# A one-core decoder step: the last tile's output projection in three banks, two weight homes freed by halves, and one expert matrix loaded later

## The chip, the cores and the metric

The kernel runs on one core of a Trainium2 chip. The metric is the time of one execution on the device in microseconds; the time of the kernel before is the median of three executions. Beside it there is one profiled execution, from which all rows below come.

## What is computed

One layer of a decoder step for 256 prompt tokens and 8 sample tokens, all in fp32. A combined input projection feeds a gated convolution, a sparse attention with an indexer, and a cross-attention; their gated sum goes through the output projection `w_o`. After that, with the 264 tokens as three row tiles (128, 128 and 8):

```
h = LN(alpha*h + mixer(h));   h = LN(alpha*h + HierMoE(h))

def hier_moe(x, w_group, b_group, w_expert, b_expert, w_up, w_down):
    lg = xt @ w_group + b_group;  le = xt @ w_expert + b_expert      # 4 groups, 8 experts in each
    # best group by lg, two best experts in it by le, gate = softmax weights; every other gate is 0
    for e in range(N_EXPERTS):                                       # 32
        hu = xt @ w_up[e]                                            # 1024 -> 2*256
        y = y + gate[:, e:e + 1] * ((silu(hu[:, :256]) * hu[:, 256:]) @ w_down[e])
```

The weights of the experts are 32 x (2 MiB up + 1 MiB down) = 96 MiB, all of which are read once.

## The kernel before, in words

**Stages.** From 0 to some 317 us of the profile the branches, the gates and the sparse attention run. Then comes the output projection with the first layer norm and the routing (some 317 to 359 us), then the experts in eight groups of four, called quads (359 to 550 us), then the second layer norm and the stores.

**Output projection.** `wo_first` multiplies tile 0 into banks 0 and 1 beside the last branch tiles. `wo_second(dh, ks)` (L1042) multiplies tile 1 (the last tile of prompt tokens) by 512 columns of `w_o` into bank 2 (dh 0) or bank 3 (dh 1), for the blocks k in `ks`; its pieces are put between the work for tiles 0 and 2 in an order written out by hand (L1071 to L1111). A finished piece raises `wo_ps`; at 3 and 4 VectorE forms h for one half of tile 1 (`residual`, L2389), at `r_ready` 3 and 4 TensorE turns it (`r_turn`, L1048), four blocks of 128 columns at a time into banks 5 and 6, and ScalarE copies it to SBUF (`h_turned`, L1680). The logits of the router for tile 1 are summed from the turned blocks (L1105 to L1108), and `lg_ps` 2 tells VectorE so.

**Routing.** VectorE takes statistics of h, centres it (`ln_centre`), forms the logits (`logit`, L2394) and the choice of experts (`route`, L2455), and scales h into the transposed store `hturn` (`ln_scale_turned`, L2379). TensorE then counts, with the matrices "tri" and ones, at which position of its expert each token stands (L1125 to L1127) and the total of each expert (L1129, six instructions), and signals both with one `pos_ps` 2. VectorE turns the positions into the gather matrix of quad 0 (`places`, `first_slots`, L2514 to L2516), takes the largest total (L2517, `cnt_read`), scales h for the residual (`ln_scale`, L2518, `h_ready` 3), and prepares the gates; `e_ready` starts ScalarE's exp (L1701), behind which on ScalarE's queue stand the two copies of gathered tokens (L1721, `first_sb` 1 and 2) that quad 0 needs. TensorE gathers with `first_part` (L1118 is its matmul; 32 instructions before the counts, 16 after), waits for `cnt_read` (L1136) and starts quad 0.

**Homes and their order.** Weight units of 2 MiB go to NWS = 10 homes in SBUF. `UNITS` is their order, six units for each quad (four up, two down); entry p lies in home p % 10. The down weights of experts 0 and 1 have no home: they lie aside, expert 1 in `down_1`, expert 0 in the halves `down_0[0]` and `down_0[1]`, three transfers that raise `aside_in` to 48. SP issues all of them in one loop (L535 on), in program order, each behind its waits. For p >= 10 the wait is `used_w`, the number of units that TensorE has used up (L562). In quad 0 home 0 and home 1 are used together by `up_half(0, 0)` (four steps r, L1209 on) and are free at the end of step 3; homes 2 and 3 by `up_half(0, 1)`. Entry 10 (two down matrices of quad 1) goes to home 0 and entry 11 (an up matrix of quad 2) to home 1. Before entry 10 SP waits for `route_ready` and issues `down_0[1]` (L559). From quad 2 to 6 the up units are whole experts, so their four homes come free only at the end of all 64 instructions of the quad's up pass.

**Quad 0 on TensorE** (L1371 on): `up_half(0, 0)`, `up_half(0, 1)`, `residual_tile(1)`, `gate_turn`, two gathers, `mid_turn`, then `down(0)` (matmuls at L1364), which waits for `aside_in` 48 (L1353) among others, then gathers, `up(1)`, and so on; `up(2)` is the L1218 pass that ends near 417 us.

The lines that the steps below touch:

```
L556  sp.dma_start(down_0[0], e0[:, 0]).then_inc(aside_in, 16)
L558  if p == NWS:
L559      sp.wait_ge(route_ready, 1)
L560      sp.dma_start(down_0[1], e0[:, 1]).then_inc(aside_in, 16)
L561  if p >= NWS:
L562      sp.wait_ge(used_w, SPENT[units[p - NWS]])
```

## Time and profile before

| | us |
|---|---|
| median of 3 runs | 571.61 |
| the three runs | 571.61, 571.46, 576.95 |
| the profiled execution | 572.16 |
| its span (what the profile covers) | 570.3 |
| granted TensorE clock, mean | 0.97 of full speed |

Engines over the span: TensorE busy 92%, VectorE 47%, ScalarE 19%, GpSimd 8%; DMA moved 162.47 MB, 285 GB/s on average. All times of rows count from the span's start. A granted clock of 1.00 is 2.4 GHz, 0.50 is 1.2 GHz. Busy shares of TensorE come from modelled ends and say little on how hard it works. MiB and KiB are powers of two (as the "KB" of the DMA answers), GB/s are decimal.

### The profile page before, as it was taken

To read this page: it belongs to the slowest core of one execution; us is meant where nothing else is said; L and a number is where in the kernel's file an instruction comes from. 1 tells how busy PE (TensorE), PEld (TensorE's weight loads), DVE (VectorE), ACT (ScalarE), POOL (GpSimd) and SP (SyncE) were. 2 spreads that over 40 slices of the span, in tenths; PEclk is the share of its full clock that TensorE was granted. 3 is DMA by queue.
4 is the path that set the end of the run, shared out by engine and by line. 5 is a ranking of instruction groups with operands and counts; after the bars stand their busy time and mean duration, and the time that the engine had idled before them with its cause. 6 is when DMAs were issued, how large, how long until landed. Compare 5 with 4: busy or idle time off the path is not lost.

```text
span 570.3 us, 9541 instructions
## 1 busy us (share of the span) xinstructions
PE 527.6 (92%) x3941; PEld 321.3 (56%) x3941; DVE 266.6 (47%) x791; ACT 107.7 (19%) x253; POOL 48.2 (8%) x64
## 2 busy tenths in 40 slices
PE   8999999998999999999999998999999795948894
PEld 4555456474577778887776557555655251512332
DVE  1272753898889976864652696411002000100016
ACT  1001112011323534322000331111111010100123
POOL 0000000001011435320000000000000000002000
PEclk9999999999999999999999998999999897989987
DMA  8990442944293568744889957799999999999972
GB/s 299 401 347 8 147 148 63 383 151 151 76 332 111 186 213 285 240 163 155 347 342 411 311 183 296 257 431 419 426 423 430 419 427 421 431 421 421 402 239 79
DMA packets 48338, 162.47 MB, mean 285 GB/s; under 512 B 6274, under 2 KB 25180, under 8 KB 39076
## 3 DMA queue, kind: packets, MB, share of 16 engines
q1 hardware_dynamic: 39472, 138.76, 62.8%
q0 software_dynamic: 3728, 14.33, 7.2%
q10 hardware_dynamic: 5092, 8.74, 4.5%
q8 instruction: 33, 0.54, 0.4%
q14 instruction: 13, 0.11, 0.1%
HBM read 159.02 MB, written 2.77 MB: 284 GB/s over the span
## 4 chain that ended last, share of the span: by engine, by line
PE 64%; DMA 14%; DVE 13%; ACTq 5%; issue 2%; ACT 1%; SPq 0%; POOLq 0%; POOL 0%; DVEq 0%
PE bank L654 14%; PE bank L833 13%; DMA ring<-in_w_up 13%; PE bank L1218 7%; PE bank L601 4%; PE bank L1248 3%; PE bank L1364 2%; ACTq L1665 2%; ACTq L1664 2%; PE bank L1188 2%; PE bank L1170 2%; DVE ring L1889 2%; DVE gates L2022 2%; PE bank L670 2%; PE bank L1287 1%
## 5 line engine op out<-in xcount | busy, mean ns | idle before, releaser
L654 PE MATMUL bank<-ring,work 128*128 128x512 f32 (+2 forms) x224 | 92.1, 547 | 0.1
L833 PE MATMUL bank<-work,ring 128*128 128x264 f32 x384 | 90.1, 390 | 0.0
L833 PEld LDWEIGHTS bank<-work,ring 128*128 128x128 f32 x384 | 71.4, 190 | 14.5 <-issue 2.5
L1218 PE MATMUL bank<-ring,work 128*32 128x512 f32 x304 | 59.0, 654 | 8.8 <-DMA proj<-in_w_up 7.6
L654 PEld LDWEIGHTS bank<-ring,work 128*128 128x128 f32 x224 | 39.5, 190 | 28.8 <-issue 25.1
L2552 DVE SCALAR_TENSOR_TENSOR work<-work,bank 128x256 f32<-128x256 f32 x8 | 3.4, 422 | 86.7 <-ACT work L1725 86.7
L1218 PE MATMUL bank<-proj,work 128*32 128x512 f32 x96 | 40.1, 646 | 4.1 <-DMA ring<-in_w_up 4.1
L2564 DVE COPY gates<-bank 128x512 f32<-128x512 f32 x7 | 4.8, 691 | 64.3 <-PE bank L1364 56.2
L1218 PEld LDWEIGHTS bank<-ring,work 128*32 128x32 f32 x304 | 15.9, 119 | 32.6 <-issue 32.5
L976 PE MATMUL bank<-work,ring 128*128 128x264 f32 x128 | 31.4, 391 | 0.7 <-ACT gates L1570 0.6
L976 PEld LDWEIGHTS bank<-work,ring 128*128 128x128 f32 x128 | 23.4, 190 | 8.7 <-issue 3.4
L1248 PE MATMUL bank<-gates,work 128*128 128x256 f32 (+1 forms) x84 | 26.5, 463 | 0.0
L1526 ACT ACTIVATE work<-bank 128x512 f32<-128x512 f32 x16 | 9.6, 598 | 75.5 <-PE bank L601 75.5
L1218 PE MATMUL bank<-extra,work 128*32 128x512 f32 x64 | 22.6, 616 | 0.9 <-issue 0.9
L2284 DVE SCALAR_TENSOR_TENSOR gates<-gates,bank 128x264 f32<-128x264 f32 x24 | 10.3, 429 | 26.9 <-PE bank L976 26.4
L1570 ACT ACTIVATE gates<-bank,gates 128x264 f32<-128x264 f32 x24 | 11.5, 480 | 59.7 <-PE bank L833 59.7
L1248 PEld LDWEIGHTS bank<-gates,work 128*128 128x128 f32 x84 | 15.8, 195 | 11.1 <-issue 8.3
L1188 PE MATMUL bank<-gates 128*128 128x256 f32 x96 | 21.8, 383 | 0.0
L1725 ACT ACTIVATE work<-bank 128x256 f32<-128x256 f32 x8 | 3.1, 384 | 90.8 <-PE bank L1218 90.8
L1869 POOL DMA_DIRECT2D ring<-in_ln_g x4 | 2.1, 517 | 203.3 <-PE bank L1218 203.3
L1188 PEld LDWEIGHTS bank<-gates 128*128 128x128 f32 x96 | 17.9, 190 | 2.4
L1218 PE MATMUL bank<-misc,work 128*32 128x512 f32 x24 | 12.1, 653 | 7.4 <-DMA ring<-in_w_up 7.0
(366 smaller groups left out, 822.9 us busy)
## 6 DMA issues: line engine op xcount, KB each, us to landing
ring<-in_w_up SPq DMA_DIRECT2D x19, 2048.0 KB, 19.8
ring<-in_w_in SPq DMA_DIRECT2D x21, 1024.0 KB, 6.7
ring<-in_w_down SPq DMA_DIRECT2D x8, 2048.0 KB, 20.2
proj<-in_w_up SPq DMA_DIRECT2D x5, 2048.0 KB, 22.5
extra<-in_w_up SPq DMA_DIRECT2D x4, 2048.0 KB, 26.4
proj<-in_w_down SPq DMA_DIRECT2D x3, 2048.0 KB, 27.0
ring<-in_w_o SPq DMA_DIRECT2D x4, 1024.0 KB, 10.1
misc<-in_w_up SPq DMA_DIRECT2D x3, 1024.0 KB, 22.4
```

The costliest lines, as they stand in the source:

```text
L601: return nc.tensor.transpose(out, in_, ident[0:n, 0:n])
L654: last = mm(bank[2 * (i % 2) + t][:, 0:w], lhs[:, k, 128 * t:128 * t + 128], rhs[:, k % 4, :], start=(k == 0), stop=(k == KT - 1))
L670: last = mm(bank[4 + i % 2][32 * j:32 * j + 32, 0:w // 4], lhs[:, k, 256:288], rhs[:, k % 4, j * w // 4:(j + 1) * w // 4], start=(k == 0), ...
L833: last = mm(b[:, 0:TOK], w[:, k, 128 * (n % 2):128 * (n % 2) + 128], xT[:, k, 0:TOK], start=(k == 0), stop=(k == KT - 1))
L976: last = mm(b[:, 0:TOK], w2[:, k % 2, 128 * n:128 * n + 128], brT[:, k0 + k, 0:TOK], start=(k == 0), stop=(k == nk - 1))
L1170: last = mm(b[:, PC * kk:PC * kk + PC], h3[:, t, 128 * k:128 * k + 128], Ssl[:, t, :], start=(t == 0), stop=(t == 2))
L1188: last = mm(bank[6 + i][:, PC * kk:PC * kk + PC], h3[:, t, 128 * k:128 * k + 128], Ssl[:, t, :], start=(t == 0), stop=(t == 2))
L1218: last = mm(bank[5][32 * j:32 * j + 32, :], xTe[q // 2 % 2][:, k, s0:s0 + CAP], up_at(q, j, k), start=(k == 0), stop=(k == KT - 1))
L1248: mm(y_part(t, part), GT[q % 2][:, 128 * t:128 * t + 128], Ysb[:, y_cols(part)], start=False, stop=False)
L1364: last = mm(bank[6 + dh][32 * j:32 * j + 32, :], hT2[:, f, 32 * j:32 * j + 32], wd, start=(f == 0), stop=(f == 1))
L1570: act.activation(gate[n], bank[gate_bank(n)][:, 0:TOK], ACT.Tanh, bias=bg[:, n:n + 1], scale=0.5)\
L1664: act.dma_start(wr[:, :, 4:36], a["w_expert"][0].rearrange("(k p) n -> p k n", p=128)).then_inc(ln_in, 16)
```

## The change

- The last tile's projection has three parts: 512 columns in bank 2, 256 in bank 3, 256 in bank 7 (`W_PARTS`). Every `wo_second(1, ...)` becomes two calls. After the last piece of part 1 (`wo_ps` 4) TensorE runs blocks 4 and 5 of part 2, turns two blocks of h, runs block 6 of part 2 (`wo_ps` 5). The residual, the statistics and the turning follow in pieces of 512, 256 and 256 columns; the last two blocks are turned into bank 2. The eight sample tokens are turned into bank 5 instead of bank 7, behind a wait for `ht_sb` 1.
- The positions raise `pos_ps` 2 ahead of the six instructions of the totals, which go to bank 3 and raise `pos_ps` 3. VectorE takes the largest total three steps later. TensorE waits for `cnt_read` behind both `up_half(0, ...)`.
- `up_half(0, 0)` raises the new `half_used` at the end of step 1. SP then issues the first halves (1 MiB each, 4 KiB runs) of entries 10 and 11, and their second halves where the whole units were. `landed` counts one more transfer for homes 0 and 1.
- `down_0[1]` is issued behind the second half of entry 11; its wait for `route_ready` goes with it. VectorE raises `route_ready` ahead of `gates_of(0)` instead of behind it.
- SP's wait ahead of entry 7 goes to `wo_ps` 5.

```diff
...
-            return 16 * (2 * uses if w == NWS - 1 else uses + 1 if w == NWS - 2 else uses)
+            return 16 * (2 * uses if w == NWS - 1 else uses + 1 if w == NWS - 2 or w < 2 and uses > 1 else uses)
...
-        zero_in = sem("zero_in")
+        zero_in, half_used = sem("zero_in"), sem("half_used")
...
+            def unit_rows(w, u, e0, half):
+                if u < UPS:
+                    s = w_up[e0 + u, :, :].rearrange("(p j r) n -> p j (r n)", p=128, j=2)
+                else:
+                    e = e0 + 2 * (u % 2)
+                    s = w_dn[e:e + 2, :, :].rearrange("j (p r) n -> p j (r n)", p=128)
+                cols = slice(1024 * half, 1024 * half + 1024)
+                sp.dma_start(wslot[w].rearrange("p (j n) -> p j n", j=2)[:, :, cols], s[:, :, cols]).then_inc(quad_in[w], 16)
+
...
-                    sp.wait_ge(wo_ps, 4)
+                    sp.wait_ge(wo_ps, 5)
...
-                    sp.wait_ge(route_ready, 1)
-                    sp.dma_start(down_0[1], e0[:, 1]).then_inc(aside_in, 16)
+                    for i in range(2):
+                        sp.wait_ge(half_used, i + 1)
+                        unit_rows(i, units[p + i] % WPQ, 4 * (units[p + i] // WPQ), 0)
...
+                elif NWS <= p < NWS + 2:
+                    unit_rows(w, n % WPQ, 4 * (n // WPQ), 1)
+                    if p == NWS + 1:
+                        sp.wait_ge(route_ready, 1)
+                        sp.dma_start(down_0[1], e0[:, 1]).then_inc(aside_in, 16)
...
-            def wo_second(dh, ks):
+            W_PARTS = ((2, 0, 512), (3, 512, 256), (7, 768, 256))
+
+            def wo_second(part, ks):
+                b, c0, w = W_PARTS[part]
...
-                    last = mm(bank[2 + dh][:, :], mT[k][:, 128:256], wo(k)[:, 512 * dh:512 * dh + 512],
-                              start=(k == 0), stop=(k == 6))
+                    last = mm(bank[b][:, 0:w], mT[k][:, 128:256], wo(k)[:, c0:c0 + w], start=(k == 0), stop=(k == 6))
...
-            def r_turn(t, half):
-                for k in range(4 * half, 4 * half + 4):
-                    last = tr(bank[5 + half][:, 128 * (k % 4):128 * (k % 4) + 128], h3[:, t, 128 * k:128 * k + 128])
+            def r_turn(t, b, k0, k1):
+                for k in range(k0, k1):
+                    last = tr(bank[b][:, 128 * (k - k0):128 * (k - k0) + 128], h3[:, t, 128 * k:128 * k + 128])
...
-            r_turn(0, 0)
-            r_turn(0, 1)
+            r_turn(0, 5, 0, 4)
+            r_turn(0, 6, 4, 8)
...
-            wo_second(1, (0, 1))
+            for part in (1, 2):
+                wo_second(part, (0, 1))
...
+            pe.wait_ge(ht_sb, 1)
...
-                last = tr(bank[7][:, 8 * k:8 * k + 8], h3[0:NS, 2, 128 * k:128 * k + 128], NS)
+                last = tr(bank[5][:, 8 * k:8 * k + 8], h3[0:NS, 2, 128 * k:128 * k + 128], NS)
...
-            wo_second(1, (2,))
+            for part in (1, 2):
+                wo_second(part, (2,))
...
-            wo_second(1, (3,)).then_inc(wo_half, 1)
+            wo_second(1, (3,))
+            wo_second(2, (3,)).then_inc(wo_half, 1)
...
-            wo_second(1, (7,))
+            for part in (1, 2):
+                wo_second(part, (7,))
...
-            r_turn(1, 0)
+            r_turn(1, 5, 0, 4)
...
+            wo_second(2, (4, 5))
...
-            r_turn(1, 1)
-
+            r_turn(1, 6, 4, 6)
+            wo_second(2, (6,)).then_inc(wo_ps, 1)
...
-            logits(1, bank[5][:, 0:36], 4, KT).then_inc(lg_ps, 1)
+            logits(1, bank[5][:, 0:36], 4, 6)
+            pe.wait_ge(r_ready, 5)
+            r_turn(1, 2, 6, 8)
+            pe.wait_ge(ht_sb, 6)
+            logits(1, bank[5][:, 0:36], 6, KT).then_inc(lg_ps, 1)
...
-            mm(bank[5][:, 64:96], ones[:, 0:128], mask[:, 64:96], start=False, stop=True)
+            mm(bank[5][:, 64:96], ones[:, 0:128], mask[:, 64:96], start=False, stop=True).then_inc(pos_ps, 1)
...
-                last = mm(bank[5][:, 96:128], ones[:, 0:128], mask[:, 32 * t:32 * t + 32], start=(t == 0), stop=(t == 2))
+                last = mm(bank[3][:, 0:32], ones[:, 0:128], mask[:, 32 * t:32 * t + 32], start=(t == 0), stop=(t == 2))
...
-            pe.wait_ge(cnt_read, 1)
...
+                        if q == 0 and b == 0 and r == 1 and j % 2 == 1:
+                            last.then_inc(half_used, 1)
...
+            pe.wait_ge(cnt_read, 1)
...
-            def h_turned(i, t):
-                for half in range(2):
-                    act.wait_ge(ht_ps, i + half)
-                    act.activation(hT[:, 4 * half:4 * half + 4, 128 * t:128 * t + 128],
-                                   bank[5 + half][:, :].rearrange("p (k n) -> p k n", k=4), ACT.Copy).then_inc(ht_sb, 1)
+            def h_turned(i, t, b, k0, k1):
+                act.wait_ge(ht_ps, i)
+                act.activation(hT[:, k0:k1, 128 * t:128 * t + 128],
+                               bank[b][:, 0:128 * (k1 - k0)].rearrange("p (k n) -> p k n", k=k1 - k0), ACT.Copy)\
+                    .then_inc(ht_sb, 1)
...
-            h_turned(1, 0)
+            h_turned(1, 0, 5, 0, 4)
+            h_turned(2, 0, 6, 4, 8)
...
-            act.activation(hT[:, :, 256:264], bank[7][:, 0:64].rearrange("p (k n) -> p k n", k=KT),
+            act.activation(hT[:, :, 256:264], bank[5][:, 0:64].rearrange("p (k n) -> p k n", k=KT),
...
-            h_turned(4, 1)
+            h_turned(4, 1, 5, 0, 4)
+            h_turned(5, 1, 6, 4, 6)
+            h_turned(6, 1, 2, 6, 8)
...
-            def residual(t, dh, s=dchain):
-                cs = slice(512 * dh, 512 * dh + 512)
-                link(V.scalar_tensor_tensor(h3[:, t, cs], bank[2 * t + dh][:, :], 0.5, xres[:, t, cs],
-                                            ALU.mult, ALU.add), s)
+            def residual(t, b, c0, w, s=dchain):
+                cs = slice(c0, c0 + w)
+                link(V.scalar_tensor_tensor(h3[:, t, cs], bank[b][:, 0:w], 0.5, xres[:, t, cs], ALU.mult, ALU.add), s)
...
-            residual(0, 0)
-            residual(0, 1, r_ready)
+            residual(0, 0, 0, 512)
+            residual(0, 1, 512, 512, r_ready)
...
-            residual(1, 0, r_ready)
-            link(V.bn_stats(stats[:, 0:6], h3[:, 1, 0:512]))
+            residual(1, 2, 0, 512, r_ready)
+            for i in range(2):
+                link(V.bn_stats(stats[:, 6 * i:6 * i + 6], h3[:, 1, 256 * i:256 * i + 256]))
...
-            residual(1, 1, r_ready)
-            link(V.bn_stats(stats[:, 6:12], h3[:, 1, 512:1024]))
-            link(V.bn_aggr(stats[:, 46:48], stats[:, 0:12]))
+            residual(1, 3, 512, 256, r_ready)
+            link(V.bn_stats(stats[:, 12:18], h3[:, 1, 512:768]))
+            dve.wait_ge(wo_ps, 5)
+            residual(1, 7, 768, 256, r_ready)
+            link(V.bn_stats(stats[:, 18:24], h3[:, 1, 768:1024]))
+            link(V.bn_aggr(stats[:, 46:48], stats[:, 0:24]))
...
-            link(V.tensor_reduce(rt[:, 143:144], bank[5][:, 96:128], AX.X, ALU.max), cnt_read)
...
+            dve.wait_ge(pos_ps, 3)
+            link(V.tensor_reduce(rt[:, 143:144], bank[3][:, 0:32], AX.X, ALU.max), cnt_read)
...
+            link(V.tensor_copy(cnt_u[:, :], rt[:, 143:144]), route_ready)
...
-            link(V.tensor_copy(cnt_u[:, :], rt[:, 143:144]), route_ready)
...
```

## Rows read from the trace of the kernel before

**Rows 1.** The page, part 4: the chain that ended last, by engine

```profile
PE 64%; DMA 14%; DVE 13%; ACTq 5%; issue 2%; ACT 1%; SPq 0%; POOLq 0%; POOL 0%; DVEq 0%
```

**Rows 2.** The chain in order of time: start us, us, what

```profile
448.29 0.28 SPq L500
...
448.62 34.04 DMA ring<-in_w_up
```

**Rows 3.** Windows: us; busy PE, PEld, DVE, ACT, POOL; clock, DMA share, GB/s

```profile
346.50:348.50 2.00, 1.75 (x16) 1.75 (x16) 1.86 (x5) 1.04 (x3) 0.00 (x0) 1.00 0.99 258
...
358.50:362.50 4.00, 3.14 (x33) 1.24 (x36) 3.49 (x14) 1.21 (x3) 0.00 (x0) 1.00 0.77 266
362.50:363.00 0.50, 0.50 (x12) 0.19 (x7) 0.16 (x2) 0.00 (x0) 0.00 (x0) 1.00 0.00 0
363.00:366.00 3.00, 3.00 (x35) 0.94 (x24) 0.00 (x0) 0.00 (x0) 0.00 (x0) 1.00 0.72 210
366.00:372.00 6.00, 6.00 (x40) 4.36 (x34) 0.84 (x2) 1.43 (x4) 0.00 (x0) 1.00 1.02 419
372.00:417.00 45.00, 43.85 (x316) 24.29 (x314) 6.05 (x13) 5.79 (x12) 0.00 (x0) 1.00 1.01 425
```

**Rows 4.** Timeline of SP: start us, us, queue, line, what it issues

```profile
357.92 0.33 SPq L496 DMA_DIRECT2D proj<-in_w_up  x1
362.46 0.33 SPq L560 DMA_DIRECT2D proj<-in_w_down  x1
...
399.30 0.43 SPq L500 DMA_DIRECT2D extra<-in_w_up  x1
417.29 0.89 SPq L516 DMA_DIRECT2D ring<-in_w_down  x2
```

**Rows 5.** DMA answers for single issues (362.46, 398.46, 398.83, 399.30): KB, us to landing

```profile
proj<-in_w_down SPq DMA_DIRECT2D x1, 512.0 KB, 3.9
...
misc<-in_w_up SPq DMA_DIRECT2D x1, 1024.0 KB, 16.2
...
gates<-in_w_up SPq DMA_DIRECT2D x1, 1024.0 KB, 18.3
...
extra<-in_w_up SPq DMA_DIRECT2D x1, 2048.0 KB, 22.7
```

**Rows 6.** Timeline of VectorE and ScalarE, 346 to 359 us

```profile
346.00 0.69 DVE L2391 SCALAR_TENSOR_TENSOR gates<-bank,work 128x512 f32<-128x512 f32 x1 [2.70 <-PE bank L1044]
...
349.43 0.25 DVE L2396 SCALAR_TENSOR_TENSOR proj<-proj,misc,bank 128x36 f32<-128x36 f32 x1
...
353.04 2.02 DVE L2380 SCALAR_TENSOR_TENSOR gates<-gates,misc,proj 128x1024 f32<-128x1024 f32 x1
355.83 0.19 DVE L2486 SCALAR_TENSOR_TENSOR cst<-bank,proj 128x32 f32<-128x32 f32 x1 [0.77 <-PE bank L1129]
...
356.38 0.19 DVE L2517 TENSOR_REDUCE proj<-bank 128x1 f32<-128x32 f32 x1
356.61 1.29 DVE L2376 SCALAR_TENSOR_TENSOR gates<-gates,misc,proj 128x1024 f32<-128x1024 f32 x1
...
358.56 0.23 ACT L1701 ACTIVATE proj<-proj 128x36 f32<-128x36 f32 x1 [9.13 <-DVE proj L1889]
```

**Rows 7.** Timeline of TensorE: the last projection piece, quad 0's start, its down pass

```profile
342.81 2.74 PE L1044 MATMUL bank<-ring,gates 128*128 128x512 f32 x6
...
359.38 0.62 PE L1218 MATMUL bank<-extra,work 128*32 128x512 f32 x2 [0.86 <-issue]
...
373.33 0.62 PE L1364 MATMUL bank<-work 128*32 128x512 f32 x2 [0.63 <-issue]
```

**Rows 8.** Windows of 2 us, columns as in rows 3

```profile
346.00:348.00 2.00, 1.25 (x12) 1.25 (x12) 1.86 (x5) 0.56 (x2) 0.00 (x0) 1.00 0.80 184
...
350.00:352.00 2.00, 2.00 (x11) 2.00 (x11) 1.71 (x10) 0.00 (x0) 0.00 (x0) 0.50 1.04 434
...
358.00:360.00 2.00, 1.14 (x13) 0.67 (x15) 1.73 (x9) 1.21 (x3) 0.00 (x0) 1.00 0.52 115
```

## Prediction

> **What bounds the kernel now.** I read the page's chain first: TensorE holds 64% of it and DMA 14% [rows 1]. In order of time the DMA share is all late: from 448 us on the chain runs through weight transfers of over 30 us each [rows 2], that is, through a queue that is long and full. So I looked at what the DMA engines did in windows. From 366 us to 417 us they moved 419 to 425 GB/s [rows 3], and nothing later in the expert stage is below that by much until the last units. From 366 us on the end is therefore a matter of bytes: it comes earlier only by as much as the queue starts earlier, and only if it never runs dry. Before 366 us there is slack: 1 MiB alone between 358.5 and 362.5 us at 266 GB/s, nothing for half a microsecond, then 210 GB/s for three [rows 3]. SP's timeline says why: the homes are full, and SP waits for `h_ready` 3 (357.92), for `route_ready` (362.46) and for the homes of quad 0 [rows 4].
>
> The full queue starts, in effect, at 364.5 us: between 363 and 366 us it moved 630 KB, which is 1.5 us of the full rate. It holds `down_0[1]` and the eleven entries 10 to 20, 22.5 MiB or 23,593 KB, before SP has to wait until 417.29 us for `up(2)` to free homes [rows 4]. By 417.0 us 630 + 2,514 + 19,125 = 22,269 KB of it have gone [rows 3], so that the rest lasts until 420.1 us. A new transfer shows its first bytes some 0.85 us behind its issue (357.92 to about 358.6, 362.46 to about 363.4) [rows 3, 4]: at 418.1. The queue is thus only 2 us from running dry there. This is the second limit, and it hangs on TensorE, which from 372 to 417 us works for 43.85 of 45 us [rows 3].
>
> **Part by part.** *Projection in three banks.* Six matmuls of 512 columns take 2.74 us with their drain [rows 7]; twelve of 256 columns cost the same to 0.2 us. Two turned blocks come ahead of the last piece (some 0.3 us), so the last signal comes at about 346.0 instead of 345.6. VectorE's residual took 0.69 us for 512 columns [rows 6]; for 256 I take 0.43, and as much for the statistics, twice 0.26 less. VectorE's later steps start 0.2 to 0.3 us sooner: the logits at 349.1 instead of 349.43 [rows 6]. The logits of the last two blocks wait for a turn and a copy and end at about the same 349.1; bounds of this edit are -0.8 and +0.6 us. It gains some 0.3 us at `ln_scale_turned`, which then ends at 354.75.
>
> *Positions ahead of totals.* VectorE waited 0.77 us at 355.83 for the six instructions of the totals [rows 6]. With the signal ahead of them, the positions are there (by 354.8 even if the clock falls as before), so `places` starts at 354.8, 1.0 us sooner. The largest total (0.19 us and a link, 356.38) [rows 6] goes behind `e_ready`: 1.25 us sooner for `ln_scale` (356.61 to 355.35), `h_ready` 3 and `e_ready`. ScalarE's exp at 358.56 [rows 6] stands ahead of the copies that quad 0 waits for, so quad 0 starts at 358.1 instead of 359.38 [rows 7]. I take 1.27 us; the ends are 0.3 (only the 0.19 and part of the wait) and 1.8. The wait for `cnt_read` behind both up halves costs nothing: VectorE has it by some 358.1, TensorE asks at 365.
>
> *Halves.* `half_used` comes two of four steps into the pass: 358.1 + 1.75 + 0.2 = 360.0 us, instead of 362.46 and 363.04 for the first issues before. SP then issues 1 MiB at 360.0 and 360.5, the second halves at 361.8 and 362.2. The 1 MiB of entry 8 goes out with `h_ready` 3, at 356.65, and is through by 361.05. The new bytes join it at 360.9, with a start that loses about 0.7 us (a lone 1 MiB took 4.0 us where the full rate asks 2.5) [rows 3]. The full queue starts in effect at 361.75, 2.75 us sooner than 364.5. That is what the change can win at most.
>
> *The aside matrix later.* `down_0[1]` used to be first in the new queue, issued at 362.46 and landed 3.9 us later, at 366.4 [rows 5], long before `down(0)` at 373.33 [rows 7]. Now 4 MiB stand ahead of it. Its data are in at 361.75 + 4,719 KB / 425 = 372.85, with 0.2 for the shorter runs 373.05. Landing lags the data: for `down_0[1]` before by 0.9 us, for the transfer of 399.30 (landed 422.0, last byte at 420.1) by 1.9 [rows 3, 5]. I take 1.5: it lands at 374.55. But `down(0)` would be ready at 373.33 - 1.27 = 372.06. TensorE waits 2.5 us, starts `down(0)` at 374.6, and all its gain is gone, with 1.27 us on top. The bounds of the landing are 373.0 and 375.5.
>
> *At 417 us.* TensorE has no slack on the way, so homes come free at 417.29 + 1.27 = 418.55. The queue, 2.75 us early, is dry at 417.35. It starts again with 0.85 us to the first byte and 0.8 lost in the start (the burst at 346.5 us moved 258 GB/s over its first 2 us [rows 3]): in effect at 420.2. Before, it ran through at 420.1. The sum is +0.1 us: 2.75 us won at the front, 2.85 lost as an idle DMA at 417 to 419. Behind this point, transfers are issued over 20 us ahead again [rows 2], and the rest keeps its length. The profiled execution's 572.16 us would be 572.26; on the median of 571.61 that is **571.7 us**. The edits to SP's wait ahead of entry 7 (+0.4 us on a transfer that quad 1 needs 25 us later), to bank 5 and to `route_ready` cost nothing; they lie beside these.
>
> The Trainium skill (DMA: Bandwidth & Descriptors, section Bandwidth) speaks against halving: it gives 341 GB/s for a transfer of 1 MB and 425 for 16 MB. The two 1 MiB transfers issued at 398.46 and 398.83 land at 414.7 and 417.1 [rows 5], 2.5 us apart, 425 GB/s: in a full queue the trace does not show that price. By the page's figure the four halves would take 2.4 us more (an estimate), and the end would be near 574.1.
>
> **Rivals.** *A, the aside matrix lands in time* (or almost). If the lag is 0.5 us and the start loses nothing, it lands at 372.8 or sooner; then `down(0)` waits under 0.8 us and homes come free at 416.0 to 416.8. Against it: 4.5 MiB at 425 GB/s alone end at 372. For it: every term of mine on this path is a guess of some tenths. The end comes 1.5 to 2.75 us sooner: 569.5.
>
> *B, slower: the wait of 2.5 us halves TensorE's clock.* In the trace the clock fell to 0.50 for 350 to 352 us after a window in which TensorE was busy for only 1.25 of 2 us, but it did not fall around 358 to 360 us, busy for 1.14 [rows 8]. If it falls once after the wait, some 3.6 us of work at half speed cost 1.8 us, the homes of `up(2)` come free at 420.3, and DMA idles as much longer: 573.5. [...] The Trainium skill (TensorE: Matmul & The Clock Gate, HAM oscillation) has the same rule: waits for DMA let the gate throttle, and the next work starts cold. It names this rival but gives it no other time.
>
> *C, slower: each half pays the price of a lone 1 MiB*, 1.5 us [rows 3], three times beyond the one counted: the aside matrix lands 4.5 us later and the end with it, 576.2. Against it: the pair in rows 5. The page's rule above is this rival's, with the smaller price.
>
> *D, the chain does not shorten*: VectorE's order of work hides the earlier positions, quad 0 starts at 359.4, and everything above comes 1.27 us later, to 573.0. Against it: the 0.77 us wait in the row.
>
> **How the numbers follow.** Forecast 0.40, A 0.28, B 0.22, C 0.04, D 0.06. The forecast's own range is 570.6 to 572.6. To hold 8 in 10 the whole range takes in most of A and B: 569.0 to 574.0. A measurement of this kernel can tell about 1% (5.7 us) from no change. No case but the upper part of C reaches it: faster 0.02, same 0.95, slower 0.03.
>
> **What would show it.** Right: quad 0's first matmul near 358.1; two SP issues near 360.0; `down(0)` behind a DMA wait of 2 to 3 us, near 374.6; DMA at full rate from 361 us; an idle DMA of about 2 us near 417 to 419 us; the end unchanged. Wrong: no wait at `down(0)` (A), a clock of 0.50 behind it (B), halves that land over 3 us apart (C), quad 0 at 359.4 (D), or an end that moves although DMA never idles.

## The result, and the profile after

The changed kernel took 578.67 us (median of four runs, 577.14 to 582.87); the kernel before, timed again beside it, took 571.54 us. The ratio is 1.0115 with a 95% interval of 1.0065 to 1.0165: slower by 1.15%, and by 7.1 us between the medians, outside the range forecast. Ratios are worked out from all fast executions of both kernels and not from the medians, so the two need not agree to the last tenth of a percent; the slow ones (of the kernel before four near 579 us and one of 2,991 us, of `e12_positions` one of 579.62 us) are left out of them. The profiled execution took 578.9 us with a span of 577.0; the one before had 572.16 and 570.3.

In the page's part 4 of the kernel after, the shares by engine hardly move against [rows 1]:

```profile
PE 63%; DVE 14%; DMA 13%; ACTq 5%; issue 2%; ACT 1%; SPq 0%; POOLq 0%; POOL 0%; DVEq 0%
```

The chain in order of time of the kernel after (start us, us, what) shows something else: it now runs through one transfer of 512 KB.

```profile
358.23 3.71 PE bank L1244 x32
361.94 0.34 SPq L509
362.33 0.82 SPq L509
363.19 13.63 DMA proj<-in_w_down
376.82 0.25 issue
377.06 5.94 PE bank L1392 x32
```

That transfer is `down_0[1]`, the aside matrix. The waits of TensorE in the kernel after (who waited for whom: us in total, times, longest) name the same:

```profile
PE bank L1392 <- DMA proj<-in_w_down: 5.5, 1, 5.5
PE bank L1515 <- DVE proj L1921: 2.8, 1, 2.8
```

The first is the wait ahead of `down(0)`: 5.5 us, where 2.5 was forecast. The second is new too; it comes in the last section.

**VectorE's chain** came out as forecast. Timeline of VectorE, ScalarE and TensorE in the kernel after, for the rows that answer to [rows 6, 7]:

```profile
346.58 0.42 DVE L2423 SCALAR_TENSOR_TENSOR gates<-bank,work 128x256 f32<-128x256 f32 x1 [0.63 <-PE bank L1062]
...
349.51 0.25 DVE L2427 SCALAR_TENSOR_TENSOR proj<-proj,misc,bank 128x36 f32<-128x36 f32 x1
...
353.12 1.99 DVE L2412 SCALAR_TENSOR_TENSOR gates<-gates,misc,proj 128x1024 f32<-128x1024 f32 x1
354.96 0.18 DVE L2517 SCALAR_TENSOR_TENSOR cst<-bank,proj 128x32 f32<-128x32 f32 x1
...
355.50 1.28 DVE L2408 SCALAR_TENSOR_TENSOR gates<-gates,misc,proj 128x1024 f32<-128x1024 f32 x1
...
357.45 0.23 ACT L1733 ACTIVATE proj<-proj 128x36 f32<-128x36 f32 x1 [7.66 <-DVE proj L1921]
...
358.23 0.62 PE L1244 MATMUL bank<-extra,work 128*32 128x512 f32 x2 [0.59 <-ACT work L1753]
```

The first position step has lost its wait of 0.77 us and starts at 354.96 instead of 355.83; `ln_scale` starts at 355.50 instead of 356.61, and quad 0 at 358.23 instead of 359.38. So 1.15 of the 1.27 us are there. The third bank gave none of it: the logits stand at 349.51 against 349.43, and the 2 us normalising step at 353.12 against 353.04. The gain also hangs on TensorE's clock, as `e1_aside_first` below shows.

**SP and its queue.** Timeline of SP in the kernel after (start us, us, queue, line, what it issues):

```profile
356.82 0.33 SPq L496 DMA_DIRECT2D proj<-in_w_up  x1
360.18 0.38 SPq L509 DMA_DIRECT2D extra<-in_w_down  x1
360.60 0.67 SPq L509 DMA_DIRECT2D ring<-in_w_up  x1
361.89 0.39 SPq L509 DMA_DIRECT2D extra<-in_w_down  x1
362.33 0.82 SPq L509 DMA_DIRECT2D ring<-in_w_up  x1
363.19 0.82 SPq L584 DMA_DIRECT2D proj<-in_w_down  x1
...
390.06 0.89 SPq L525 DMA_DIRECT2D ring<-in_w_down  x2
...
423.32 0.89 SPq L525 DMA_DIRECT2D ring<-in_w_down  x2
```

The issues stand where the forecast had them (360.0, 360.5, 361.8, 362.2). Their landings don't. The DMA answers of the kernel after for entry 8 (issued at 356.82) and for the aside matrix (363.19), KB and us to landing:

```profile
proj<-in_w_up SPq DMA_DIRECT2D x1, 1024.0 KB, 7.4
proj<-in_w_down SPq DMA_DIRECT2D x1, 512.0 KB, 13.6
```

Entry 8 took 4.8 us before, when nothing followed it for 4.5 us; here, with halves behind it 3.4 us later, it takes 7.4 and lands at 364.2. The halves are not what set this: over all profiles it took 4.8 to 7.6 us, 7.6 in `e3_whole_last`, where nothing was issued behind it for 5.1 us, and 5.6 in `e5_busy_wait`, with the same halves 3.4 us behind it. By bytes it was nearly through when the forecast had it so: from 357.5 to 361.5 us the engines moved 1,056 KB, about its size. The aside matrix lands at 376.82; [rows 5] had it in 3.9 us. Windows of the kernel after, columns as in [rows 3]:

```profile
361.00:367.00 6.00, 6.00 (x46) 1.94 (x37) 1.52 (x6) 0.39 (x1) 0.00 (x0) 1.00 0.89 250
...
372.00:376.00 4.00, 0.00 (x0) 0.00 (x0) 0.00 (x0) 0.00 (x0) 0.00 (x0) 0.87 1.07 437
376.00:380.00 4.00, 2.94 (x16) 0.91 (x20) 0.00 (x0) 0.00 (x0) 0.00 (x0) 0.50 1.03 436
...
388.00:392.00 4.00, 4.00 (x41) 1.44 (x37) 0.00 (x0) 0.00 (x0) 0.00 (x0) 1.00 0.73 240
...
417.00:425.00 8.00, 8.00 (x69) 3.14 (x62) 0.84 (x2) 0.77 (x2) 0.00 (x0) 1.00 0.65 254
```

and the same windows of the kernel before, where they are not in [rows 3]:

```profile
388.00:392.00 4.00, 4.00 (x18) 3.19 (x19) 2.12 (x5) 1.26 (x3) 0.00 (x0) 1.00 0.97 412
...
417.00:425.00 8.00, 7.27 (x41) 5.50 (x41) 0.84 (x2) 2.24 (x5) 0.00 (x0) 1.00 1.00 422
```

Read them in order. From 361 to 367 us the DMA engines are busy for 0.89 of the time but move 250 GB/s, 1,500 KB, which is 3.5 us of the full rate: the queue starts in effect at 363.5, one microsecond sooner than before. From 372 to 376 TensorE does nothing at all, while the queue runs full. Then it works at a granted clock of 0.50, its lower level of 1.2 GHz. The groups of instructions between 370 and 384 us in the kernel after (count | busy us, mean ns of one | idle before) give the price:

```profile
L1392 PE MATMUL bank<-ring,work 128*32 128x512 f32 x16 | 5.9, 911 | 0.0
```

and the same group in the kernel before:

```profile
L1364 PE MATMUL bank<-ring,work 128*32 128x512 f32 x16 | 3.6, 596 | 0.0
```

The busy times are 5.9 and 3.6 us (an fp32 matmul shows as two records, and `down(0)` has 32 in all, of which this group has half), so the clock cost 2.3 us. `down(0)` starts at 377.06 instead of 373.33, 3.73 us later, and with 2.3 us on top the homes of `up(2)` should come free 6.03 us later. They do: 423.32 against 417.29 [rows 4]. The queue has all but run dry at 421 us (66 GB/s from there to 423) and is empty from 423 to 424.2 us. It has also run thin at 388 to 392, since another home came free at 390.06 instead of 384.03; that point was in no part of the forecast.

The sum: homes free at 423.32, and 1.65 us from there to the queue in effect (the forecast's own term) make 424.97 against 420.1, so 4.9 us. Measured, the combine of the samples at the head of the last stage starts at 563.92 against 558.40, 5.5 us later. The last stage takes 0.9 us more (10.54 against 9.65 us from there to the issue of the last store), together 6.4 of the 6.7 us between the spans.

### The profile page after: what moved, and what is told of

Same layout as the page of the kernel before. It is cut to its first block, busy times and chain, and to the rows that moved or that the text cites. A ratio compares the mean times of both kernels' runs of the same rounds, so it can differ in the third digit from the quotient of the medians.

```text
span 577.0 us, 9582 instructions
## 1 busy us (share of the span) xinstructions
PE 529.9 (92%) x3957; PEld 322.7 (56%) x3957; DVE 267.2 (46%) x794; ACT 107.7 (19%) x254; POOL 48.9 (8%) x64
## 4 chain that ended last, share of the span: by engine, by line
PE 63%; DVE 14%; DMA 13%; ACTq 5%; issue 2%; ACT 1%; SPq 0%; POOLq 0%; POOL 0%; DVEq 0%
PE bank L669 13%; PE bank L848 13%; PE bank L1244 8%; DMA proj<-in_w_up 6%; PE bank L616 4%; DMA ring<-in_w_up 4%; PE bank L1276 3%; PE bank L1392 3%; DMA proj<-in_w_down 2%; ACTq L1694 2%; ACTq L1693 2%; PE bank L1214 2%; PE bank L1196 2%; DVE ring L1921 2%; DVE gates L2054 2%
## 5 line engine op out<-in xcount | busy, mean ns | idle before, releaser
L1244 PE MATMUL bank<-ring,work 128*32 128x512 f32 x304 | 59.4, 655 | 7.2 <-DMA proj<-in_w_up 6.7
L1244 PE MATMUL bank<-extra,work 128*32 128x512 f32 x64 | 25.2, 688 | 0.6 <-ACT work L1753 0.6
L1276 PEld LDWEIGHTS bank<-gates,work 128*128 128x128 f32 x84 | 15.8, 195 | 11.1 <-issue 8.3
L1244 PE MATMUL bank<-misc,work 128*32 128x512 f32 x24 | 14.7, 769 | 7.8 <-DMA ring<-in_w_up 7.4
L1392 PE MATMUL bank<-ring,work 128*32 128x512 f32 x112 | 20.4, 639 | 0.7 <-ACT work L1767 0.7
```

The lines of the kernel that those rows point to most:

```text
L1244: last = mm(bank[5][32 * j:32 * j + 32, :], xTe[q // 2 % 2][:, k, s0:s0 + CAP], up_at(q, j, k), start=(k == 0), stop=(k == KT - 1))
L1276: mm(y_part(t, part), GT[q % 2][:, 128 * t:128 * t + 128], Ysb[:, y_cols(part)], start=False, stop=False)
L1392: last = mm(bank[6 + dh][32 * j:32 * j + 32, :], hT2[:, f, 32 * j:32 * j + 32], wd, start=(f == 0), stop=(f == 1))
```

## The experiments

All ratios are against the kernel before, timed beside the run on the same chip; its median was 573.42 us beside the first four runs, 571.77 beside the next four and 572.52 beside the last four. Each run has one profile. The theories have letters in the expectations: T, that the whole loss is the late aside matrix and what follows from it; H, that the halves themselves are slow; K, that the halved clock behind the wait costs time of its own; Q, that the home freed at 417 us is a second limit, at which a queue that started sooner runs dry. (C is there that the edits of the chain cost the time, not rival C of the prediction; W, that the clock costs nothing at the end.)

**The place of the aside matrix.** Four kernels side by side: the halves and the chain are in or out, the aside matrix ahead of the new transfers or behind them.

*Halves and chain in, aside matrix first* (`e1_aside_first`):

```diff
                 if p == NWS:
+                    sp.wait_ge(route_ready, 1)
+                    sp.dma_start(down_0[1], e0[:, 1]).then_inc(aside_in, 16)
+                if p == NWS:
                     for i in range(2):
                         sp.wait_ge(half_used, i + 1)
...
                     unit_rows(w, n % WPQ, 4 * (n // WPQ), 1)
-                    if p == NWS + 1:
-                        sp.wait_ge(route_ready, 1)
-                        sp.dma_start(down_0[1], e0[:, 1]).then_inc(aside_in, 16)
```

> Only the place of the aside matrix is undone: SP waits for route_ready and issues it ahead of the two first halves (route_ready comes near 360.2, as half_used does, so the halves go out some 0.4 us later). Theory T (all of the loss is the late aside matrix: TensorE's wait at down(0), the half clock behind it, and the idle DMA that follows when homes come free late): the matrix lands near 364.5, down(0) starts near 372.2 without a wait, no idle DMA near 390 or 421, time 569 to 571, below the kernel before. Rival H (the halves themselves load slowly, 266 GB/s from 361 to 367 us): no wait at down(0), but the queue is behind by 2 us: 572 to 575. Rival C (something in the chain edits costs the 6 us): 577 or more, unchanged.

573.0 us, ratio 0.9996 (0.996 to 1.0031). The transfer was issued at 360.41 and landed 5.0 us later; `down(0)` waited for no DMA and started at 373.34. Windows of this run:

```profile
388.00:392.00 4.00, 4.00 (x18) 3.19 (x19) 2.12 (x5) 1.26 (x3) 0.00 (x0) 1.00 0.95 401
...
420.00:424.00 4.00, 3.41 (x17) 2.86 (x15) 0.00 (x0) 1.38 (x3) 0.00 (x0) 1.00 0.98 408
```

Both thin stretches are gone with the wait. Moving this one transfer takes back the whole loss. The mechanism is T's, but the time is H's: against the kernel before, nothing is won, although the halves went out sooner.

One reason is in the profile, and the forecast had no place for it. The last 16 gathers ahead of quad 0, timeline of TensorE in this run and in the changed kernel:

```profile
355.81 3.64 PE L1145 MATMUL bank<-gates 128*128 128x128 f32 x16 [0.94 <-DVE gates L2520]
```

```profile
355.61 2.02 PE L1145 MATMUL bank<-gates 128*128 128x128 f32 x16 [0.94 <-DVE gates L2520]
```

The same work took 3.64 us instead of 2.02, at a granted clock of 0.50 from 356 to 358 us, and quad 0 starts at 359.39, as in the kernel before. Of the twelve profiles of kernels with the earlier positions, six have the slow gathers (`e1`, `e6`, `e7`, `e8`, `e10`, `e11`: 3.3 to 3.6 us) and six have not (2.02 us); the two profiles of kernels without the earlier positions (the one before, `e4_before_last`) have not. Where they come, quad 0 starts 0.7 to 1.0 us later, and most of the chain's 1.15 us is gone. From 354 to 356 us TensorE was busy for 1.72 us before and for only 1.05 in this run, but for 1.06 in the changed kernel as well, whose clock stayed up; what decides it is open.

*The chain alone: no halves, aside matrix first* (`e2_whole_first`), the part that ought to be a pure gain; entries 10 and 11 are whole units again and `half_used` is not raised:

```diff
                 if p == NWS:
-                    for i in range(2):
-                        sp.wait_ge(half_used, i + 1)
-                        unit_rows(i, units[p + i] % WPQ, 4 * (units[p + i] // WPQ), 0)
+                    sp.wait_ge(route_ready, 1)
+                    sp.dma_start(down_0[1], e0[:, 1]).then_inc(aside_in, 16)
```

> Aside matrix first and entries 10 and 11 whole again, as in the kernel before; of the change only the chain part is left (three banks, positions ahead of totals, cnt_read later). T: down(0) starts near 372.1, 1.2 us sooner than before; the queue starts 1.0 us sooner; time 570.3 to 571. H: the same, and clearly below e1. C: 577.

571.93 us, ratio 0.9983 (0.9955 to 1.0011). `down(0)` started at 372.42, 0.9 us sooner than in [rows 7], and homes came free at 416.37, but the time can't be told from that before, nor from `e1_aside_first` (the intervals overlap).

*Chain in, whole units, aside matrix last* (`e3_whole_last`), and *nothing of the change but the aside matrix last* (`e4_before_last`), whose edit to the kernel before is shown; `e3_whole_last` has the same lines in the changed kernel, with the halves taken out:

```diff
                 if p == NWS:
-                    sp.wait_ge(route_ready, 1)
-                    sp.dma_start(down_0[1], e0[:, 1]).then_inc(aside_in, 16)
...
                     expert_unit(w, n % WPQ, 4 * (n // WPQ))
+                if p == NWS + 1:
+                    sp.wait_ge(route_ready, 1)
+                    sp.dma_start(down_0[1], e0[:, 1]).then_inc(aside_in, 16)
```

> Entries 10 and 11 whole, but the aside matrix behind entry 11, as in the changed kernel. T: SP issues the aside matrix near 362.7, 4 MiB of whole units stand ahead of it; they start 1.5 us later than the halves did, so it lands near 376.5 to 377.5, TensorE waits 4.5 to 5.5 us at down(0), time 576 to 579, as the changed kernel. H (it is the halves that made it land late): whole units load at full rate, it lands at 374 to 375, wait of 2 to 3 us, time 572 to 574.

> The kernel before with one edit: the aside matrix behind entry 11. It is issued near 363.9 behind 4 MiB. T: it lands near 377.5 to 378.5 against a need at 373.3, so TensorE waits 4 to 5 us there, the clock may fall to half behind it; homes of up(2) come free at 422 to 424 and DMA idles; time 574 to 579. H: 4 MiB at 425 GB/s from 364.5 put it at 376, a wait of 2.5 us, time 572 to 573. C: no change from 571.5.

`e3_whole_last`: 578.01 us, ratio 1.0079 (1.0046 to 1.0112). `e4_before_last`: 576.74 us, ratio 1.0059 (1.0028 to 1.0089). Both are T's wait and time, with landings at 375.9 and 376.6, somewhat sooner than T had them. Waits of TensorE in `e4_before_last`:

```profile
PE bank L1364 <- DMA proj<-in_w_down: 4.5, 1, 4.5
```

and its SP timeline and windows (columns as in [rows 3]):

```profile
362.77 0.38 SPq L516 DMA_DIRECT2D extra<-in_w_down  x1
363.20 0.47 SPq L500 DMA_DIRECT2D ring<-in_w_up  x1
363.71 0.43 SPq L573 DMA_DIRECT2D proj<-in_w_down  x1
```

```profile
374.00:378.00 4.00, 1.11 (x8) 0.45 (x12) 0.00 (x0) 0.00 (x0) 0.00 (x0) 0.67 0.95 385
...
420.00:424.00 4.00, 4.00 (x38) 1.22 (x28) 0.00 (x0) 0.38 (x1) 0.00 (x0) 1.00 0.39 160
```

The move alone, made to the kernel before, reproduces the wait, the lower clock and the dry queue, and costs 0.59% (the whole change cost 1.15%; the intervals just overlap). Taken back in the changed kernel, it takes the loss away. So that it is the cause is shown in both directions.

The pair says more, and here theory H holds in part. From the first new issue to the aside matrix's landing it took 13.9 us in `e4_before_last`, 14.2 in `e3_whole_last`, and 16.6 in the changed kernel. In that profile the halves go out 1.4 us sooner than the whole units of `e3_whole_last`, and the same bytes land 1 us later. Three later profiles with the same halves and the matrix last are `e9_after_again`, `e5_busy_wait` and `e10_busy_again`. The rates in GB/s, microsecond by microsecond, from 0.85 us behind the first new issue:

| profile | entries 10, 11 | GB/s, 1st to 6th us | lost against 425 | issue to landing |
|---|---|---|---|---|
| changed kernel | halves | 119, 295, 279, 229, 250, 332 | 2.5 us | 16.6 us |
| `e9_after_again` | halves | 148, 279, 283, 217, 250, 332 | 2.5 us | 17.2 us |
| `e5_busy_wait` | halves | 135, 291, 291, 254, 295, 385 | 2.1 us | 15.6 us |
| `e10_busy_again` | halves | 139, 279, 299, 233, 287, 414 | 2.1 us | 15.5 us |
| `e3_whole_last` | whole | 147, 328, 410, 401, 434, 500 | 0.8 us | 14.2 us |
| `e4_before_last` | whole | 156, 279, 442, 434, 426, 459 | 0.8 us | 13.9 us |

The queue is at its full rate in the third microsecond with whole units and only in the sixth or seventh with halves. That costs 1.3 to 1.7 us, and what halving wins at the issue it loses in the queue's start. Two things differ between the rows, the size of the transfers and how close behind entry 8 the first one is issued (3.4 to 4.2 us with halves, 5.1 with whole units); no run separates them. From the seventh microsecond on, halves move at the full rate too.

**Is it the place behind all four, or behind any?** `e6_aside_mid` puts the aside matrix between the first and the second halves:

```diff
                         unit_rows(i, units[p + i] % WPQ, 4 * (units[p + i] // WPQ), 0)
+                    sp.wait_ge(route_ready, 1)
+                    sp.dma_start(down_0[1], e0[:, 1]).then_inc(aside_in, 16)
...
-                    if p == NWS + 1:
-                        sp.wait_ge(route_ready, 1)
-                        sp.dma_start(down_0[1], e0[:, 1]).then_inc(aside_in, 16)
```

> The changed kernel with the aside matrix behind the two first halves instead of behind all four. By the landings of the changed kernel (second first half at 370.4) it lands near 371.7, just ahead of the need near 372.0. Theory T: no or at most 0.5 us of wait at down(0), no half clock, 571 to 573, as with the matrix first. If the loss grew with the distance in the queue and not by the need (rival H), it would be half of the full loss: 574.5 to 576.

572.34 us, ratio 1.0014 (0.9987 to 1.0041). It landed 9.4 us after its issue, and TensorE did not wait for it. That is T. So 2 MiB ahead of it are hidden, 4 MiB are not.

**Another queue.** `e11_aside_act` leaves SP's order as changed, without the aside matrix, which ScalarE issues:

```diff
+            act.wait_ge(route_ready, 1)
+            act.dma_start(down_0[1], ...).then_inc(aside_in, 16)
```

> The changed kernel, with the aside matrix issued by ScalarE's DMA queue behind route_ready (near 360.3) instead of by SP behind the four halves; SP's order of the halves stays. Theory T (only the matrix's own landing counts): on another queue of the same engines it shares the rate with the halves, so it lands 3 to 6 us behind its issue, at 364 to 367, no wait at down(0), 571 to 572.5. Rival (whatever stands in front of it in any queue counts, or the halves suffer by the same amount): it lands after 372 and TensorE waits.

571.8 us, ratio 1.0008 (0.9974 to 1.0041). Timeline of ScalarE, and the DMA answer for it:

```profile
358.91 0.35 ACTq L1753 DMA_DIRECT2D proj<-in_w_down  x1
```

```profile
proj<-in_w_down ACTq DMA_DIRECT2D x1, 512.0 KB, 4.5
```

It lands at 363.4. Counted from the issue of entry 8 that is 12 us sooner than behind the halves (7.9 us for 20.0), and the loss is gone, as T had it. But it also went out 3.0 us sooner by the same count, 0.8 us ahead of the first half (issued at 359.73), and first in SP's own queue it took only 3.6 to 5.3 us in the six profiles that have it there (3.9 in [rows 5]). So the run shows that an early landing is enough, and not what a second queue does for a transfer that is issued behind the halves. The Trainium skill (DMA: Bandwidth & Descriptors, Rules for kernel authors) says that spreading transfers over the engines' queues brings no bandwidth; no run here shows otherwise.

**What the clock costs.** `e5_busy_wait` and, timed again later, `e10_busy_again` put five matmuls of 512 columns (ten records) ahead of the wait, whose product nobody reads (added work, nothing left out), so that TensorE is busy in it. `e9_after_again` is the changed kernel itself, beside the second.

```diff
                 if q == 0:
+                    for _ in range(5):
+                        mm(bank[5][:, :], ones[:, 0:128], ..., start=True, stop=True)
                     pe.wait_ge(aside_in, 48)
```

> The changed kernel with five matmuls of 512 columns (4.3 us of work whose result is never used) between the other waits of down(0) and the wait for the aside matrix, so that TensorE is busy instead of idle while the matrix is on its way. They start near 371.9 and end near 376.3. Theory K (the half clock is a good part of the loss): the matrix still lands near 376.8, down(0) starts near 377.1 but at a clock of 1.00 and ends near 380.8 instead of 383.0; homes come free 2 to 2.5 us sooner; 576 to 577. Rival W (the wait alone counts, the clock costs nothing at the end since DMA sets it): as the changed kernel, 578 to 579.

> The changed kernel as it is, for a comparison on one chip with the next run. Both theories: 577 to 579, a ratio of 1.010 to 1.013 to the kernel before.

> The kernel of e5 again (the changed kernel with five idle matmuls of 512 columns ahead of the wait for the aside matrix), beside the changed kernel. Its one profile showed down(0) at a clock of 1.00 in 3.6 us against 5.9 us. Theory K: 2 to 4 us below e9, 574 to 576. Rival W: within 1 us of e9.

`e5_busy_wait` took 577.79 us, ratio 1.0101 (1.0046 to 1.0156); `e10_busy_again` 576.08 us, 1.0064 (1.0031 to 1.0097); `e9_after_again` 578.07 us, 1.0122 (1.0077 to 1.0166). Timeline of TensorE in `e5_busy_wait`:

```profile
374.08 4.53 PE L1382 MATMUL bank<-work,cst 128*128 128x512 f32 x10 [0.57 <-ACT work L1751]
378.54 0.62 PE L1395 MATMUL bank<-work 128*32 128x512 f32 x2
```

Each matmul of `down(0)` has its full-speed 0.62 us, and the granted clock is 1.00. From the issue of the first half to the homes of `up(2)` it took 63.1 us in the changed kernel, 62.9 in `e9_after_again` and 60.4 in both busy ones, so the traces give 2.6 to 2.8 us back; most of it is the clock, and `down(0)` also started 0.5 to 1.0 us sooner behind the first half's issue. In time, `e10_busy_again` and `e9_after_again`, run beside each other, differ by 2.0 us in the medians and 0.6% in the ratios, though the intervals overlap; `e5_busy_wait` gave back 0.1% of the changed kernel's 1.15%. So the clock's part is seen in the traces and likely in the time, 2.3 of 7.1 us or about a third of the loss; the rest is the wait itself. K holds as a part, its size in the medians stays open. The Trainium skill (TensorE: Matmul & The Clock Gate, HAM oscillation) has this rule, that work behind a wait for DMA starts at the lower clock, and the traces agree: 0.50 from 376 to 380 us here, and behind the waits of 4.5, 4.8 and 6.0 us in `e4_before_last`, `e3_whole_last` and `e9_after_again` too.

**The limit at 417 us.** `e7_halves_q2` and `e8_whole_q2` load quad 2's up matrices in units instead of whole, so that homes come free sooner, with halves and with whole units, the aside matrix first in both (the edit of `WHOLE` is shown; the others are those of `e1_aside_first` and `e2_whole_first`, and in `e7_halves_q2` entry 11's halves are read as rows of two experts):

```diff
-WHOLE = range(2, QUADS - 1)
+WHOLE = range(3, QUADS - 1)
```

> Aside matrix first, halves kept, and quad 2 no longer as whole experts (its up units are loaded as row halves of two experts, as in quads 0 and 1), so that its first two homes come free 3.5 us sooner, near 413.8 instead of 417.3. Theory Q (with the matrix in time, what the earlier queue wins is lost again because the queue runs dry before up(2) frees its homes): no dip of the DMA rate near 417 us, and the time falls by what the queue won, 1 to 2.5 us below the kernel before: 569 to 570.5. Rival (the halves win nothing to begin with, since the start of the queue is slow whatever is asked of it): 571 to 572, as with whole units.

> As the run before, but entries 10 and 11 whole: the chain part of the change and quad 2 by halves. Q: the queue starts 0.9 us sooner than in the kernel before and no longer runs dry: 570.3 to 571. The difference to the run before is what the halves are worth. Rival (nothing runs dry at 417): no difference to the kernel before beyond 0.3 us.

571.51 us, ratio 1.0008 (0.9976 to 1.004), and 573.21 us, ratio 1.0018 (0.9992 to 1.0044). First the window from 416 to 420 us of `e2_whole_first`, then that of `e7_halves_q2`:

```profile
416.00:420.00 4.00, 4.00 (x22) 3.17 (x19) 0.84 (x2) 1.07 (x3) 0.00 (x0) 1.00 0.95 373
```

```profile
416.00:420.00 4.00, 4.00 (x22) 3.19 (x19) 0.84 (x2) 1.09 (x3) 0.00 (x0) 1.00 0.98 412
```

With quad 0 a microsecond sooner the DMA engines dip to 373 GB/s there (422 before), and with homes free at 412.93 they don't: the limit that Q names exists. But the dip is worth only 0.5 us (373 for 425 GB/s over 4 us), and taking it away brought nothing that these intervals show: in time both rivals came nearer than Q. `e7_halves_q2` and `e8_whole_q2` differ by 0.1%, within the noise, so halves are worth nothing that can be seen. Both profiles have the slow gathers ahead of quad 0.

**The positions alone.** `e12_positions` is the kernel before with the earlier signal of the positions, the totals in bank 3, the count read later and `route_ready` ahead of the gates, and no third bank; the lines for the positions and the totals are shown:

```diff
-            mm(bank[5][:, 64:96], ones[:, 0:128], mask[:, 64:96], start=False, stop=True)
+            mm(bank[5][:, 64:96], ones[:, 0:128], mask[:, 64:96], start=False, stop=True).then_inc(pos_ps, 1)
...
-            link(V.tensor_reduce(rt[:, 143:144], bank[5][:, 96:128], AX.X, ALU.max), cnt_read)
             ln_scale(ytmp, 1, lnb, h_ready)
...
+            dve.wait_ge(pos_ps, 3)
+            link(V.tensor_reduce(rt[:, 143:144], bank[3][:, 0:32], AX.X, ALU.max), cnt_read)
```

> The kernel before with one part of the change alone: positions signalled ahead of the totals, totals in bank 3, cnt_read and the largest total later, route_ready ahead of the gates. Projection, homes and aside matrix as before. The positions part is worth the 0.77 us wait and most of the 0.19 us operation: quad 0 starts 0.9 us sooner against entry 8's need, down(0) near 372.4; if the queue starts as much sooner and is not dry at 417, 570.7; if the end does not move, the gain is lost in the queue at 417 (theory Q), 571.5.

572.62 us, ratio 0.9999 (0.9963 to 1.0034). Entry 8 went out at 356.83, as in the changed kernel (356.82), and quad 0 started at 358.24: the positions alone give the chain's whole gain. The time does not show it: the end did not move, as in the second of the two forecasts. The executions of the kernel before that count in these ratios spread from 568.9 to 576.4 us, so a gain of under a microsecond is beyond these runs. No version here beats the kernel before.

## Why the prediction was wrong

*What bounds the kernel*: held. The end hung on when the queue starts and on where it runs dry, and the home of `up(2)` is the second limit.

*The chain*: 1.15 us for 1.27, quad 0 at 358.23 for 358.1. The terms within it were shared out wrongly: the third bank was to give 0.3 us and gave none, the positions gave all. That the number came so close is in part luck: in half of the profiles with the earlier positions a clock of 0.50 at the gathers takes 0.7 to 1.0 us of it back, a cost that the forecast put at nothing.

*The halves' issues*: held to 0.2 us.

*The failed step is the queue's start*, "a start that loses about 0.7 us". The row cited for it gives 1.5 us (a lone 1 MiB took 4.0 where the full rate asks 2.5), and why 0.7 was taken is not said. 0.7 is about what whole units lose (0.8 us in two profiles). With halves, 361 to 367 us moved 3.5 us' worth: 2.5 us lost, in effect 363.5 instead of 361.75, and 2.1 to 2.5 in three more profiles. The difference, 1.75 us, passed into the landing of the aside matrix, and another 0.5 us is the lag of data and landing (363.5 + 11.1 for 4,719 KB at 425 gives 374.6, it landed at 376.82: 2.2 us where the 0.2 and the 1.5 were taken). So the landing came 2.3 us behind 374.55, outside the bounds of 373.0 and 375.5. Both bounds had kept the start at 361.75; its own uncertainty, the largest, was missing from them.

*The wait at `down(0)`*: the right place and mechanism, 5.5 us for 2.5. *Rival B* then held as well, behind the longer wait: clock 0.50, 2.3 us for its 1.8. I had priced it for a landing at 374.55 only. The later landing and the clock belong to one case, and its chance was not small. *Rival C* was right that halves cost something, 1.3 to 1.7 us more than whole units and not 4.5, and wrong in how: by their issues and the DMA answers (7.7, 9.8, 11.1 and 13.2 us) the four halves land at 367.9, 370.4, 373.0 and 375.5, each about 2.5 us behind the last, which is 1 MiB at 425 GB/s. What they paid was paid once, ahead of the first landing. *Rivals A and D* fell; a late quad 0, D's sign, shows in six later profiles, but by the clock and not by VectorE's order of work.

*At 417 us*: the formula was right. With the measured home (423.32) it gives 4.9 us of delay, against 5.5 us measured ahead of the last stage. The forecast of +0.1 was right as arithmetic and had the wrong input. The thin stretch at 388 to 392 us was not seen, because I followed only the home at which TensorE's 1.3 us would matter.

*"The rest keeps its length"*: the last stage took 0.9 us longer, see below.

## What to carry to other kernels

When a transfer is moved back in a queue, compare its landing with the need of its reader, and put the uncertainty of the queue's start into the bounds of that landing; if the margin is a few microseconds, the small transfer with the near reader goes first. In this kernel a wait of 4.5 to 6.0 us on TensorE cost twice, once as idle time and once as a clock of 0.50 behind it, and again at every point where the homes that it freed late left the queue dry. Halving a home's load brought the issue forward by 1.4 us and the bytes not at all. And an earlier start is won only where the clock stays up behind it: look at the granted clock of that stretch in more than one profile.

## What the runs showed of the hardware beyond that

- With halves in front the DMA engines' busy share was 0.89 over 361 to 367 us and the rate only 250 GB/s; with 0.95 they moved 373 in `e2_whole_first` at 416 to 420 us. So the busy share alone does not say how fast a queue moves. Why a queue of halves starts so slowly stays open.
- The same 1 MiB transfer (entry 8) landed between 4.8 and 7.6 us behind its issue in the profiles here, and what was issued behind it does not explain which.
- 512 KB on ScalarE's queue landed in 4.5 us, issued 3.4 us behind entry 8 and 0.8 us ahead of the halves on SP's queue.
- In all eleven profiles with the third bank (the changed kernel's and ten of these runs) TensorE pauses for 2.5 to 2.9 us at the head of the last stage, `PE bank L1515` in the waits above, although what it is said to wait for was done long before. In `e4_before_last`, in `e12_positions` and before there is a wait of 0.8 us there, behind the second matmul of the group, and no such pause. In `e2_whole_first`, timeline of TensorE:

```profile
557.58 0.64 PE L1281 MATMUL bank<-gates,work 128*32 128x256 f32 x8
560.73 1.55 PE L1507 MATMUL bank<-proj,cst 128*128 128x512 f32 x3 [2.50 <-DVE proj L1913]
```

From the combine of the samples to the last store it took 9.65 to 9.67 us in the three profiles without the pause and 10.2 to 10.6 in nine with it. In the other two, `e9_after_again` and `e10_busy_again`, it took 11.9 and 12.6 us: there the granted clock fell to 0.50 behind the pause. The pause stands where TensorE's program branches around code that is not run here, and the changed kernel has sixteen more matmul records (3,957 for 3,941); that these shift the fetching of instructions is argued, not shown. One transfer of the instruction queue falls into this stretch in the kernel before as well as in the changed one, so its mere presence does not tell them apart.
